# Sums over partitions of modulation products: ones as the moving operand, or the products moving past a pattern of ones

## The chip, the cores and the metric

The kernel runs on one core of one Trainium2 chip. The metric is the device time of one launch in microseconds (us); lower is better. All numbers are fp32; the large matrix products are done in three terms, each operand split into a high part and a low part.

## The reference, cut to what matters

Two transformer blocks run one after the other. The second one is conditioned: in each of its two layers a vector `c` (for the latents) and a vector `c_ctx` (for the context) are multiplied with a large matrix, and the 6144 results of each are the shifts, scales and gates of that layer.

```python
def ada_params(cvec, w, b):                       # w: (1024, 6144)
    return jnp.split(jax.nn.silu(cvec) @ w + b, 6, axis=-1)

for l in range(DEPTH):                            # DEPTH = 2
    sh1, sc1, g1, sh2, sc2, g2 = ada_params(c, ada_w[l], ada_b[l])
    csh1, csc1, cg1, csh2, csc2, cg2 = ada_params(c_ctx, ada_w[l], ada_b[l])
    h_lat = modulate(x, norm_g[l, 0], sh1, sc1)
    h_ctx = modulate(ctx, norm_g[l, 0], csh1, csc1)
    ...
```

The context's last four results of layer 1 are never used, so they are not computed.

## The kernel before

The kernel is one hand-written stream of instructions for each engine, with semaphores between them: `pe.wait_ge(dve_done, at("dve", name))` lets TensorE wait for the VectorE instruction that carries that name. Activations lie feature-major: 128 features on the partitions, tokens along the row.

The feed-forward networks take their weights in chunks through two slots. SyncE loads a chunk into `raw`, ScalarE rounds it to `WH` (line 828), GpSimd forms the rest `WL` (line 757), and TensorE multiplies. A network goes through four quarters of 6, 6, 6 and 4 tiles (`QUARTERS`). In a quarter, each tile has a gate and an up product (`streamed`, lines 2958, 2959, 2963), VectorE multiplies the two to `FH` and `FL` (lines 1782 to 1785), and then eight products of the down projection follow in four steps of two (`lowered`, lines 3178, 3179, 3183, the loop over `k` in steps of 2), whose results VectorE adds up (lines 1796 and 1798).

The modulation vectors are worked out beside two of these networks: layer 0 beside the network `b0`, layer 1 beside the network `t`. Each layer is cut into 12 pieces of 512 result columns (`modulations`: `l`, `block`, and the vectors `vs`). Sixteen pieces are done for both vectors, eight (of layer 1) for one. A piece comes as two halves of the 1024 rows, one DMA of 1 MB each. VectorE multiplies each 128x512 tile by a column of the vector and adds it to `acc` (`modulation`, lines 1756 and 1758), so that 128 partial products for each result remain, one on each partition. TensorE then sums over the partitions (`sums`, line 3114): for each of the 4 blocks of 128 results and each vector, the 128x128 partial products are the stationary operand, and one column of ones moves past them. The result is one column of a PSUM bank, `M[1]` and `S[1]` by turns, results on the partitions, and VectorE adds the bias and writes it to `mod` (`modulated`, line 1771). An fp32 matmul shows as two records in the trace.

The order is fixed by chunk: `half_of` says after which chunk VectorE does which half; TensorE sums piece p after the chunk of the second half of piece p + 1, and the last two pieces of a layer are flushed in the last of the network's quarters that has halves (`flush`), after step `k == 4` of its down projection: quarter 3 for `b0`, quarter 2 for `t`. There, sums of pieces 10 and 11 (22 and 23) are called; piece 10 has been summed by then in `b0`, and piece 22 in `t`.

Of the kernel before, what the change touches and what calls it, by code (L numbers as in the profile page):

```python
# [26 lines left out]
AX = mybir.AxisListType  # L27

P = 128
T = 512  # L30
TC = 256
D = 1024
# [139 lines left out]
def build(nc, a, out, scratch, known):  # L172
# [4 lines left out]
    with ctx:  # L177
# [51 lines left out]
        conv, g_ab, g_qk, gate_b = keep("conv", [P, 3, 4]), keep("g_ab", [P, KD]), keep("g_qk", [P, 2]), keep("gate_b", [16, 1])  # L229
        mlast = keep("mlast", [64, 1])  # L230
        dec = keep("dec", [P, 2, 4])
        mids, steps = keep("mids", [P, 2, T // CHUNK + 2]), keep("steps", [P, 4, TC // CHUNK])
        arena = (cursor[0] + 63) // 64 * 64

# [262 lines left out]
        for name, places in (("b0", (some, most, most, range(4))), ("t", (range(8),) * 3)):  # L497
            for q, slots in enumerate(places):
                for j in slots:
                    half_of[first[f"{name}.gu{q}"] + j] = len(half_of)  # L500
            flush[name, len(places) - 1] = len(half_of) // 2 - 2
        modulations = [(0, b, (0, 1)) for b in range(12)] + [(1, b, (0,)) for b in range(4, 12)] + [(1, b, (0, 1)) for b in range(4)]
        assert len(half_of) == 2 * len(modulations)

        def piece(p):

            return (*modulations[p], (adaw0, adaw1), acc)
# [1161 lines left out]
        def _(dve):  # L1669
# [69 lines left out]
            def modulation(c):  # L1739

                if c not in half_of:
                    return
                h = half_of[c]
                if h % 2 == 0 and h >= 4:
                    modulated(h // 2 - 2)
                l, block, vs, weights, sums = piece(h // 2)
                b = h // 2 % 2
                dve.wait_ge(ada_loaded[h % 2], 16 * (h // 2 + 1))
                dve.wait_ge(dve_done, here())
                for k in range(KD // 2):  # L1750
                    for i, v in enumerate(vs):
                        col = cvec[:, KD // 2 * (h % 2) + k, v:v + 1]
                        if k:
                            dve.wait_ge(dve_done, here() - (len(vs) - 1))
                        if k == 0 and h % 2 == 0:
                            V.tensor_scalar(sums[:, b, i, :], weights[h % 2][:, k, :], col, None, ALU.mult).then_inc(dve_done, did("dve", f"ada.{h}"))
                        else:
                            V.scalar_tensor_tensor(sums[:, b, i, :], weights[h % 2][:, k, :], col, sums[:, b, i, :], ALU.mult, ALU.add)\  # L1758
                                .then_inc(dve_done, did("dve", f"ada.{h}"))

            mods = [0]

            def modulated(p):

                if p < mods[0]:
                    return
                mods[0] = p + 1
                l, block, vs, _, _ = piece(p)
                nv = len(vs)
                dve.wait_ge(pe_done, at("pe", f"ada.sum{p}"))  # L1770
                V.tensor_tensor(mod[:, l, 4 * block:4 * block + 4, vs[0]:vs[0] + nv], (M[1], S[1])[p % 2][:, 0:4 * nv].rearrange("p (b v) -> p b v", b=4),
                                ada_b[:, l, 4 * block:4 * block + 4, vs[0]:vs[0] + nv], ALU.add).then_inc(dve_done, did("dve", f"ada.mod{p}"))

            def feed_forward(n, total, N=T, FH=FH, FL=FL, silu=silu, fresh=False, between=iter(()), last=None):
                for q, count in enumerate(QUARTERS):
# [12 lines left out]
                    for k in range(KD):  # L1788
# [9 lines left out]
                            V.tensor_tensor(total[:, k, :], total[:, k, :], bank, ALU.add).then_inc(dve_done, did("dve", f"{n}.down{q}.{k}"))  # L1798
                        if k % 2 and count == 6:
                            modulation(first[f"{n}.dn{q}"] + k // 2)  # L1800
                        if k == 5 and (n, q) in flush:
                            modulated(flush[n, q])
                            modulated(flush[n, q] + 1)
                        if k % 2:
                            if last and count == 4 and k < KD - 1:
                                for j in EARLY[last].get(k // 2, ()):
# [156 lines left out]
            def bounds_high():  # L1963
# [9 lines left out]
                dve.wait_ge(dve_done, here())  # L1973
                V.tensor_scalar(lb1[:, :, :], lb[:, :, :], -1.0, 1.0, ALU.mult, ALU.add).then_inc(dve_done, did("dve", "lb1"))
                V.tensor_scalar(lbn[:, :, :], lb[:, :, :], -1.0, None, ALU.add).then_inc(dve_done, did("dve", "lbn"))

            def turning():

# [962 lines left out]
        def _(pe):  # L2941
# [160 lines left out]
            def sums(p):  # L3102

                if p < summed[0]:
                    return
                summed[0] = p + 1
                _, _, vs, _, part = piece(p)
                nv = len(vs)
                pe.wait_ge(dve_done, at("dve", f"ada.{2 * p + 1}"))
                if p >= 2:  # L3110
                    pe.wait_ge(dve_done, at("dve", f"ada.mod{p - 2}"))
                for b in range(4):
                    for v in range(nv):
                        last = mm((M[1], S[1])[p % 2][:, nv * b + v:nv * b + v + 1], part[:, p % 2, v, b * P:b * P + P], ones[:, 0:1], start=True, stop=True)
                last.then_inc(pe_done, did("pe", f"ada.sum{p}"))

            def feed_forward(n, N=T, FH=FH, FL=FL, freed=(), between=iter(())):
                X = features(hH, hL, N)
# [9 lines left out]
                for q, count in enumerate(QUARTERS):  # L3128
# [17 lines left out]
                    for k in range(0, KD, 2):  # L3146
# [9 lines left out]
                            tally.also("pe", f"used.{c}")  # L3156
                        if count == 6:
                            sums_after(c)
                        if k == 4 and (n, q) in flush:
                            sums(flush[n, q])  # L3160
                            sums(flush[n, q] + 1)
                        next(between, None)
                for _ in between:
                    pass
# [1031 lines left out]
```

## Time and profile before

| what | value |
|---|---|
| median of 3 runs | 3110.86 us (3107.64 to 3112.96) |
| the profiled execution's own time | 3109.12 us |
| its span, first to last instruction | 3107.3 us |
| mean granted TensorE clock | 0.989 of full speed |
| TensorE busy with matmuls | 3023.5 us, 97% of the span |
| VectorE / ScalarE / GpSimd busy | 55% / 38% / 40% |

The profile is of one execution. PE is TensorE's matmuls, PEld its weight loads, which overlap them, DVE is VectorE, ACT ScalarE, POOL GpSimd. A matmul's duration in the trace runs to the end of its pipeline, so the durations of a stream of matmuls overlap; what one costs is the distance from one to the next, which the chain of work that ended last gives. The page's share of 128x1 matmuls is therefore not what they cost.

### The profile page before, as it was taken

How to read it: one execution, taken by the hardware profiler on the slowest of the kernel's cores; microseconds unless marked ns; L12 is line 12 of the kernel's file. 1: busy time of each engine (PE TensorE's matmuls, PEld its weight loads, DVE VectorE, ACT ScalarE, POOL GpSimd, SP SyncE). 2: the span in 40 equal slices, each digit the busy share in tenths (PEclk: the TensorE clock that was granted, in tenths of full speed). 3: DMA queues.
4: the chain of work that ended last, by engine and by line, in shares of the span. 5: the costliest groups of instructions: out<-in, count | busy, mean ns of one | idle time of the engine just before them, and what ended most of it. 6: DMA issues, size and time to landing. Idle time of an engine off the chain costs nothing.

```text
span 3107.3 us, 41472 instructions
## 1 busy us (share of the span) xinstructions
PE 3023.5 (97%) x16448; PEld 2534.3 (82%) x16448; DVE 1702.9 (55%) x2822; ACT 1182.1 (38%) x1826; POOL 1235.6 (40%) x584
## 2 busy tenths in 40 slices
PE   8999999999999999999999999999999999999999
PEld 7658888886589888778888998878888789878887
DVE  4545676845463553655328866676684457442113
ACT  4643212235445333234336645532223335332222
POOL 4314444533266333333444554444444330244442
PEclk9999999999999999999999999999999999999999
DMA  8214554622245223223333333345653220123331
GB/s 132 65 50 124 166 162 137 182 65 65 70 129 151 83 72 92 82 68 106 112 102 99 113 113 107 128 132 180 190 157 114 76 68 2 41 72 102 99 95 68
DMA packets 480433, 323.87 MB, mean 104 GB/s; under 512 B 102520, under 2 KB 447744, under 8 KB 479728
## 3 DMA queue, kind: packets, MB, share of 16 engines
q1 hardware_dynamic: 475472, 309.60, 34.0%
q10 hardware_dynamic: 2656, 6.30, 0.5%
q0 software_dynamic: 2112, 5.32, 0.5%
q8 instruction: 131, 2.15, 0.3%
q14 instruction: 62, 0.51, 0.1%
HBM read 315.90 MB, written 5.24 MB: 103 GB/s over the span
## 4 chain that ended last, share of the span: by engine, by line
PE 89%; DVE 6%; ACT 2%; issue 1%; POOL 1%; DMA 0%; DVEq 0%; ACTq 0%; POOLq 0%
PE G L2949 13%; PE G L2958 13%; PE G L2959 12%; PE G L2963 12%; PE G L3178 6%; PE G L3179 6%; PE G L3183 6%; PE G L2976 3%; PE G L4097 1%; PE G L3748 1%; PE SS L3306 1%; PE G L3410 1%; PE G L3343 1%; PE SS L2949 1%; POOL WL L757 1%
## 5 line engine op out<-in xcount | busy, mean ns | idle before, releaser
L757 POOL TENSOR_TENSOR WL<-raw,WH 128x1024 fp32r<-128x1024 f32 (+1 forms) x520 | 1192.6, 2316 | 1747.6 <-ACT WH L828 1747.5
L828 ACT ACTIVATE WH<-raw 128x1024 fp32r<-128x1024 f32 (+1 forms) x520 | 492.6, 995 | 596.4 <-PE G L3183 404.2
L2958 PE MATMUL G<-hH,WH 128*128 128x512 f32 x1520 | 595.1, 391 | 0.7 <-ACT xtok L1562 0.7
L2959 PE MATMUL G<-hL,WH 128*128 128x512 f32 x1520 | 591.9, 389 | 0.0
L2963 PE MATMUL G<-hH,WL 128*128 128x512 f32 x1520 | 359.9, 389 | 0.0
L2958 PEld LDWEIGHTS G<-hH,WH 128*128 128x128 f32 x1520 | 285.4, 188 | 61.4 <-ACT xtok L1562 0.9
L2963 PEld LDWEIGHTS G<-hH,WL 128*128 128x128 f32 x1520 | 285.3, 188 | 59.2
L2959 PEld LDWEIGHTS G<-hL,WH 128*128 128x128 f32 x1520 | 285.4, 188 | 58.5
L1758 DVE SCALAR_TENSOR_TENSOR acc<-adaw,cvec,acc 128x512 f32<-128x512 f32 x280 | 280.1, 1053 | 4.2
L1782 DVE TENSOR_TENSOR FH<-silu,G 128x512 fp32r<-128x512 f32 x44 | 30.3, 688 | 245.4 <-PE G L2963 191.0
L2949 PE MATMUL G<-hH,WH 128*128 128x512 f32 (+1 forms) x416 | 161.5, 388 | 0.0
L2949 PE MATMUL G<-hL,WH 128*128 128x512 f32 (+1 forms) x416 | 158.8, 382 | 0.0
L2949 PE MATMUL G<-hH,WL 128*128 128x512 f32 (+1 forms) x416 | 158.8, 382 | 0.0
L3178 PE MATMUL G<-FH,WH 128*128 128x512 f32 x352 | 140.9, 400 | 0.0
L3179 PE MATMUL G<-FL,WH 128*128 128x512 f32 x352 | 138.9, 394 | 0.0
L908 ACT ACTIVATE silu<-G 128x512 f32<-128x512 f32 x44 | 26.4, 600 | 277.9 <-PE G L2963 269.0
L1782 DVE TENSOR_TENSOR m_FH<-m_silu,G 128x512 fp32r<-128x512 f32 x22 | 15.1, 688 | 189.3 <-PE G L2963 183.8
L2949 PEld LDWEIGHTS G<-hL,WH 128*128 128x128 f32 x416 | 80.0, 192 | 15.0 <-issue 0.7
L2949 PEld LDWEIGHTS G<-hH,WH 128*128 128x128 f32 x416 | 79.8, 192 | 14.9 <-issue 0.7
L2949 PEld LDWEIGHTS G<-hH,WL 128*128 128x128 f32 x416 | 79.8, 192 | 14.9
L3183 PE MATMUL G<-FH,WL 128*128 128x512 f32 x352 | 85.8, 391 | 0.0
L2958 PE MATMUL G<-c_nH,WH 128*128 128x256 f32 x336 | 84.2, 290 | 0.0
(825 smaller groups left out, 6040.3 us busy)
## 6 DMA issues: line engine op xcount, KB each, us to landing
raw<-ffn_w_in_in SPq DMA_DIRECT2D x264, 256.0 KB, 3.4
adaw<-ada_w_in SPq DMA_DIRECT2D x48, 1024.0 KB, 5.3
raw<-ab_w_in_in SPq DMA_DIRECT2D x128, 256.0 KB, 3.0
raw<-ffn_w_out_in SPq DMA_DIRECT2D x96, 256.0 KB, 3.0
raw<-w_gate_in SPq DMA_DIRECT2D x88, 256.0 KB, 3.3
raw<-w_up_in SPq DMA_DIRECT2D x88, 256.0 KB, 3.4
raw<-w_down_in SPq DMA_DIRECT2D x64, 256.0 KB, 3.0
raw<-w_in_in SPq DMA_DIRECT2D x40, 256.0 KB, 3.3
```

Source lines behind the costliest of these rows:

```text
L757: nc.gpsimd.tensor_tensor(WL[c % 2][:, cut], raw[c % 2][:, cut], WH[c % 2][:, cut].bitcast(F32), ALU.subtract)\
L828: nc.scalar.activation(WH[c % 2][:, cut], raw[c % 2][:, cut], ACT.Copy).then_inc(weights_hi, 1)
L1758: V.scalar_tensor_tensor(sums[:, b, i, :], weights[h % 2][:, k, :], col, sums[:, b, i, :], ALU.mult, ALU.add)\
L1782: V.tensor_tensor(FH[:, j, :], silu[:, t % 2, :], up, ALU.mult).then_inc(dve_done, did("dve", f"{n}.FH{t}"))
L2949: last = mm(dst, x, y, start=(k == 0 and j == 0), stop=(k == K - 1 and j == 2))
L2958: mm(dst, view(WH[c % 2], k), high, start=(k == 0 and not (joint and i)), stop=False)
L2959: mm(dst, view(WH[c % 2], k), low, start=False, stop=False)
L2963: last = mm(dst, view(WL[c % 2], k), X(k)[0], start=False, stop=(k == K - 1 and not (joint and i == 0)))
L2976: last = mm(dst, x, y, start=(k == order[0] and j == 0 and not (joint and i)), stop=(k == K - 1 and j == 2 and not (joint and i == 0)))
L3178: mm(dst, part(WH, k, cols, o), high, start=(k == 0 and not (joint and i)), stop=False)
L3179: mm(dst, part(WH, k, cols, o), low, start=False, stop=False)
L3183: last = mm(dst, part(WL, k, cols, o), X(k)[0], start=False, stop=(k == count - 1 and not (joint and i == 0)))
```

## The change

A tile `pick` of 128 x 43 elements holds zeros and one column of ones, column 11. Its 32 columns from `11 - block` on are a stationary operand of 32 columns whose column number `block` is ones. The partial products now move: for each vector and each half (256 columns) of a piece, one matmul adds the sums into row `block` of a strip of 32 rows of the bank `M[1]`, and zeros into its other rows. The four strips are (vector, half) = rows 0, 32, 64 and 96. The bank gathers all 12 pieces of a layer; `start` is set on a strip's first piece and `stop` on its last. At the end of a layer VectorE copies the 128x256 bank into `acc` (`modulated_rows`), TensorE turns it with two transposes into `S[1]` (`turned_sums`), and VectorE adds the bias in four instructions (`modulated`). The 24 single additions and their waits are gone; in `b0` the last sums come after step `k == 2` of the down projection and the turn after `k == 4`, in `t` after `k == 4` and `k == 6`.

```diff
+PICKED = 12
+        pick = keep("pick", [P, PICKED + 31])
-            flush[name, len(places) - 1] = len(half_of) // 2 - 2
+            flush[name, len(places) - 1] = (len(half_of) // 2 - 2, 2 if name == "b0" else 4)
 # VectorE
                 if h % 2 == 0 and h >= 4:
-                    modulated(h // 2 - 2)
+                    dve.wait_ge(pe_done, at("pe", f"ada.sum{h // 2 - 2}"))
+            def modulated_rows(p):
+
+                dve.wait_ge(pe_done, at("pe", f"ada.sum{p}"))
+                V.tensor_copy(acc[:, 0, 0, 0:2 * P], M[1][:, 0:2 * P]).then_inc(dve_done, did("dve", f"ada.rows{p}"))
 
             def modulated(p):
 
-                l, block, vs, _, _ = piece(p)
-                nv = len(vs)
-                dve.wait_ge(pe_done, at("pe", f"ada.sum{p}"))
-                V.tensor_tensor(mod[:, l, 4 * block:4 * block + 4, vs[0]:vs[0] + nv], (M[1], S[1])[p % 2][:, 0:4 * nv].rearrange("p (b v) -> p b v", b=4),
-                                ada_b[:, l, 4 * block:4 * block + 4, vs[0]:vs[0] + nv], ALU.add).then_inc(dve_done, did("dve", f"ada.mod{p}"))
+                l = piece(p)[0]
+                pe_name = f"ada.turned{p}"
+                dve.wait_ge(pe_done, at("pe", pe_name))
+                by_block = lambda t: t[:, l, :, :].rearrange("p (b h c) v -> p c v h b", h=2, c=2)
+                for c in range(2):
+                    turned = S[1][:, c * P:c * P + P].rearrange("p (v h b) -> p v h b", v=2, h=2)
+                    for v in range(2):
+                        V.tensor_tensor(by_block(mod)[:, c, v], turned[:, v, :, 0:PICKED], by_block(ada_b)[:, c, v], ALU.add)\
+                            .then_inc(dve_done, did("dve", f"ada.mod{l}"))
 ...
-                        if k == 5 and (n, q) in flush:
-                            modulated(flush[n, q])
-                            modulated(flush[n, q] + 1)
+                        if (n, q) in flush:
+                            p, step = flush[n, q]
+                            if k == step + 1:
+                                modulated_rows(p + 1)
+                            if k == step + 3:
+                                modulated(p + 1)
 ...
+            V.memset(pick[:, :], 0.0).then_inc(dve_done, did("dve", "pick.0"))
+            dve.wait_ge(dve_done, here())
+            V.memset(pick[:, PICKED - 1:PICKED], 1.0).then_inc(dve_done, did("dve", "pick"))
 # TensorE, in sums(p)
                 pe.wait_ge(dve_done, at("dve", f"ada.{2 * p + 1}"))
-                if p >= 2:
-                    pe.wait_ge(dve_done, at("dve", f"ada.mod{p - 2}"))
-                for b in range(4):
-                    for v in range(nv):
-                        last = mm((M[1], S[1])[p % 2][:, nv * b + v:nv * b + v + 1], part[:, p % 2, v, b * P:b * P + P], ones[:, 0:1], start=True, stop=True)
+                chosen = pick[:, PICKED - 1 - block:PICKED + 31 - block]
+                for v in vs:
+                    same = [i for i, m in enumerate(modulations) if m[0] == l and v in m[2]]
+                    for h in range(2):
+                        r = 64 * v + 32 * h
+                        last = mm(M[1][r:r + 32, 0:2 * P], chosen, part[:, p % 2, v, h * 2 * P:h * 2 * P + 2 * P], start=(p == same[0]), stop=(p == same[-1]))
                 last.then_inc(pe_done, did("pe", f"ada.sum{p}"))
+
+            def turned_sums(p):
+
+                pe.wait_ge(dve_done, at("dve", f"ada.rows{p}"))
+                for c in range(2):
+                    last = nc.tensor.transpose(S[1][:, c * P:c * P + P], acc[:, 0, 0, c * P:c * P + P], ident[:, :])
+                last.then_inc(pe_done, did("pe", f"ada.turned{p}"))
 ...
-                        if k == 4 and (n, q) in flush:
-                            sums(flush[n, q])
-                            sums(flush[n, q] + 1)
+                        if (n, q) in flush:
+                            p, step = flush[n, q]
+                            if k == step:
+                                sums(p)
+                                sums(p + 1)
+                            if k == step + 2:
+                                turned_sums(p + 1)
```

## Rows read from the trace of the kernel before

**Rows 1.** The page: span, TensorE's busy time, chain by engine.

```profile
span 3107.3 us, 41472 instructions
PE 3023.5 (97%) x16448; PEld 2534.3 (82%) x16448; DVE 1702.9 (55%) x2822; ACT 1182.1 (38%) x1826; POOL 1235.6 (40%) x584
...
PE 89%; DVE 6%; ACT 2%; issue 1%; POOL 1%; DMA 0%; DVEq 0%; ACTq 0%; POOLq 0%
```

**Rows 2.** Busy time by stretch: networks `b0` and `t`, then a quarter's end.

```profile
core 0: us, PE busy (x) PEld busy (x) DVE busy (x) ACT busy (x) POOL busy (x), PEclk, DMA share, GB/s
225.00:625.00 400.00, 399.46 (x1874) 333.30 (x1873) 282.40 (x332) 98.08 (x122) 178.16 (x85) 1.00 0.51 154
2060.00:2345.00 285.00, 285.00 (x1321) 237.64 (x1320) 209.49 (x235) 64.56 (x81) 127.07 (x56) 1.00 0.58 177
...
420.00:460.00 40.00, 40.00 (x193) 33.44 (x192) 38.67 (x43) 8.75 (x10) 19.09 (x9) 1.00 0.60 178
```

**Rows 3.** Chain, a piece of two vectors: start us, us, what.

```profile
324.70 1.68 PE MM L3114 x16
326.38 0.34 PE G L3178
326.73 0.23 PE G L3179
```

**Rows 4.** Chain, a piece of one vector.

```profile
2110.78 0.79 PE SS L3114 x8
2111.57 0.34 PE G L3178
```

**Rows 5.** Line 3114 by instruction: min/median/max ns, first and last start.

```profile
L3114 PEld LDWEIGHTS MM<-ones,acc x160: 187/192/193, 324.3 to 2335.1; 128*128 128x128 f32 x160
...
L3114 PEld LDWEIGHTS SS<-ones,acc x160: 187/192/193, 342.6 to 2345.2; 128*128 128x128 f32 x160
```

**Rows 6.** Timeline of TensorE: full width, then strips of 64.

```profile
146.94 1.88 PE L3306 MATMUL MM<-kT,qT 128*128 128x512 f32 x4
148.75 1.94 PE L3410 MATMUL G<-pt,vtok 128*64 128x512 f32 x8
```

**Rows 7.** Chain, other fp32 matmuls: 512 columns at full width.

```profile
145.81 1.30 PE SS L3306 x3
```

**Rows 8.** Chain, strips of 64 columns (line 3286), then full width.

```profile
112.64 1.02 PE MM L3286 x16
113.66 0.67 PE G L2949 x2
```

**Rows 9.** Line 3286 by instruction.

```profile
L3286 PEld LDWEIGHTS MM<-w_sT,vg x64: 132/137/137, 110.5 to 734.9; 128*64 128x64 f32 x64
```

**Rows 10.** Timeline of TensorE: 32 rows each, four banks.

```profile
1667.42 0.38 PE L3729 MATMUL SS<-t_va,rstd 32*128 32x128 f32 x2
1667.43 0.38 PE L3729 MATMUL MM<-t_va,rstd 32*128 32x128 f32 x2
```

**Rows 11.** Chain, four transposes inside a stream of matmuls.

```profile
2728.06 0.44 PE G L3055 x4
2728.50 1.16 PE G L2976 x5
```

**Rows 12.** Timelines at the end of `t`, quarter 2.

```profile
2315.55 0.69 DVE L1782 TENSOR_TENSOR t_FH<-ht,G 128x512 fp32r<-128x512 f32 x1 [1.92 <-PE G L2963]
...
2326.53 0.16 DVE L1771 TENSOR_TENSOR mod<-SS,ada_b 128x8 f32<-128x8 f32 x1
2326.80 3.79 DVE L1756 TENSOR_SCALAR acc<-adaw,cvec 128x512 f32<-128x512 f32 x2
...
2336.26 7.07 DVE L1758 SCALAR_TENSOR_TENSOR acc<-adaw,cvec,acc 128x512 f32<-128x512 f32 x8
...
2343.63 1.84 PE L3114 MATMUL SS<-ones,acc 128*128 128x1 f32 x16
```

**Rows 13.** Timelines at the end of `b0`, quarter 3.

```profile
609.80 8.70 DVE L1758 SCALAR_TENSOR_TENSOR acc<-adaw,cvec,acc 128x512 f32<-128x512 f32 x8
...
620.21 0.42 PE L3178 MATMUL G<-FH,WH 128*128 128x512 f32 x1
...
632.33 0.69 DVE L1798 TENSOR_TENSOR xT<-xT,G 128x512 f32<-128x512 f32 x1 [1.54 <-PE G L3183]
```

**Rows 14.** Timeline of VectorE: its first instruction.

```profile
9.12 0.69 DVE L2022 COPY xT<-G 128x512 f32<-128x512 f32 x1 [9.12 <-PE G L3422]
```

**Rows 15.** Groups by line: a copy of the new copy's shape.

```profile
L2912 DVE COPY ptj<-G 128x256 f32<-128x256 f32 x32 | 13.5, 423 | 8.4 <-PE G L4087 6.8
```

More of the change, by code:

```diff
@@ L1759, in modulation @@
                                 .then_inc(dve_done, did("dve", f"ada.{h}"))
-            mods = [0]
+            def modulated_rows(p):
+                dve.wait_ge(pe_done, at("pe", f"ada.sum{p}"))
+                V.tensor_copy(acc[:, 0, 0, 0:2 * P], M[1][:, 0:2 * P]).then_inc(dve_done, did("dve", f"ada.rows{p}"))
             def modulated(p):
-                if p < mods[0]:
-                    return
-                mods[0] = p + 1
-                l, block, vs, _, _ = piece(p)
-                nv = len(vs)
-                dve.wait_ge(pe_done, at("pe", f"ada.sum{p}"))
-                V.tensor_tensor(mod[:, l, 4 * block:4 * block + 4, vs[0]:vs[0] + nv], (M[1], S[1])[p % 2][:, 0:4 * nv].rearrange("p (b v) -> p b v", b=4),
-                                ada_b[:, l, 4 * block:4 * block + 4, vs[0]:vs[0] + nv], ALU.add).then_inc(dve_done, did("dve", f"ada.mod{p}"))
+                l = piece(p)[0]
[7 more added lines that the diff above has]
+                            .then_inc(dve_done, did("dve", f"ada.mod{l}"))
             def feed_forward(n, total, N=T, FH=FH, FL=FL, silu=silu, fresh=False, between=iter(()), last=None):
@@ L3106, in sums @@
                 summed[0] = p + 1
-                _, _, vs, _, part = piece(p)
-                nv = len(vs)
+                l, block, vs, _, part = piece(p)
                 pe.wait_ge(dve_done, at("dve", f"ada.{2 * p + 1}"))
-                if p >= 2:
-                    pe.wait_ge(dve_done, at("dve", f"ada.mod{p - 2}"))
-                for b in range(4):
-                    for v in range(nv):
-                        last = mm((M[1], S[1])[p % 2][:, nv * b + v:nv * b + v + 1], part[:, p % 2, v, b * P:b * P + P], ones[:, 0:1], start=True, stop=True)
-                last.then_inc(pe_done, did("pe", f"ada.sum{p}"))
+                chosen = pick[:, PICKED - 1 - block:PICKED + 31 - block]
[4 more added lines that the diff above has]
+                        last = mm(M[1][r:r + 32, 0:2 * P], chosen, part[:, p % 2, v, h * 2 * P:h * 2 * P + 2 * P], start=(p == same[0]), stop=(p == same[-1]))
+                last.then_inc(pe_done, did("pe", f"ada.sum{p}"))
+            def turned_sums(p):
[3 more added lines that the diff above has]
+                last.then_inc(pe_done, did("pe", f"ada.turned{p}"))
             def feed_forward(n, N=T, FH=FH, FL=FL, freed=(), between=iter(())):
```

## The prediction

> **What bounds the kernel now.** I read the page first, for the engine that is nearly always busy: TensorE, 97% of the span, and 89% of the chain that ended last [rows 1]. An average hides stages, so I then asked for the busy times of the two stretches in which modulation pieces are summed. In `b0` TensorE is busy 399.5 of 400 us, in `t` 285.0 of 285, at a granted clock of 1.00, which is the upper of the two levels (2.4 GHz) [rows 2]. The reader is to see that nothing TensorE waits for shows there: every microsecond less on it is a microsecond less in all, until another engine is late. GpSimd and ScalarE are at half load or less in both stretches; VectorE is at 71 to 74%, but 38.7 of 40 us at the end of a quarter, so it is the one that could be late next.
>
> **What goes.** A matmul of one moving column looks as if it cost nothing. It doesn't: its 128x128 stationary operand has to be loaded, 187 to 192 ns a load [rows 5], and the loads overlap each other only in part. The chain gives what a burst costs: 16 records take 1.68 us, and the matmul behind them 0.34 us where its neighbours take 0.23 [rows 3], together 1.79 us. The bursts of one vector take 0.79 + 0.11 = 0.90 us [rows 4]. There are 320 records [rows 5]: 16 bursts of 16 and 8 of 8. So 16 x 1.79 + 8 x 0.90 = 28.6 + 7.2 = 35.8 us of TensorE go.
>
> **What comes.** A piece of two vectors is now four matmuls (eight records) of 256 moving columns, each into its own strip of 32 result rows; a piece of one vector is two matmuls (four records). An fp32 record of 512 columns takes 1.30 / 3 = 0.43 us [rows 7], so one of 256 takes 0.215 us. Done one behind the other, eight would be 1.72 us, about what goes. All hangs on whether the strips run side by side.
>
> The trace has strips of 64. Four records at full width take 1.88 us from start to end; eight into two strips, with the same 512 columns, take 1.94 [rows 6]. So two strips run at once. It has no strips of 32 result rows, but it has four matmuls of 32 contraction rows each, on four banks, which start within 0.01 us of each other [rows 10]. Two records of each bank stand together only in the merged view; what it shows is that four small matmuls can be in the array at once. I take four strips at once, so two slots of 0.215 us: 0.43 us.
>
> The way in and out costs extra. Line 3286 does 16 records of 128 columns in pairs: eight slots of 0.43 / 4 = 0.108 us are 0.86 us. It takes 1.02 us, and the two matmuls behind it 0.67 us, where two take 0.46 [rows 8]: 1.23 us in all, so 0.37 us for entering and leaving strips. A burst is then 0.37 + 0.43 = 0.80 us, and the same for one vector, whose two strips also need two slots. 24 x 0.80 = 19.2 us. **TensorE gains 35.8 - 19.2 = 16.6 us**, almost all in the 16 large bursts (0.99 each, against 0.10 in the small ones).
>
> The bounds of a burst of two vectors: 0.43 us if entering cost nothing, 0.37 + 8 x 0.215 = 2.09 us if nothing overlapped. I stay at 0.80 since rows 6 and 8 are the nearest in kind: the same two-record fp32 matmuls into strips.
>
> The Trainium skill ("TensorE: Matmul & The Clock Gate", Measured speedup vs the span model) has 3.07x for four row strips and 2.38x for three column strips. By 3.07x, as an estimate, the eight records would take 0.56 us in place of 0.43, and the change would gain 2 us less. The two strips here give 2 x 1.88 / 1.94 = 1.94x.
>
> **The turn.** Two transposes a layer stand in TensorE's stream. Four in such a stream cost 0.44 us, and the matmuls behind run at 0.23 [rows 11]; two are between 0.22 and 0.44. I take 0.3 us, 0.6 for both layers. The copy before them (0.42 us by a copy of its shape [rows 15]) and the four additions (0.16 us each, as the 0.16 of those that go [rows 12]) are VectorE's. In `t` they lie in front of the next quarter. In `b0` VectorE still waits 1.54 us for TensorE behind the place where they are put [rows 13], which covers them; without that cover they would cost 0.42 + 4 x 0.16 - 2 x 0.16 = 0.7 us. The two transposes wait for the copy, but a whole step of the down projection stands between, so I cost that wait at nothing. The memsets of `pick` come while VectorE idles for its first 9.12 us [rows 14]: nothing.
>
> **A stall that appears.** The gain makes TensorE early, and one of its waits has no slack. In `t` the last sums wait for the last half of piece 23. VectorE has worked without a gap since 2315.55 and ends that half at 2336.26 + 7.07 = 2343.33; TensorE's burst starts at 2343.63 [rows 12]. Two bursts lie on TensorE between 2315 and there (pieces 21 and 22), each 0.99 us shorter, so it arrives at 2341.65. VectorE loses the addition at 2326.53, 0.27 us with its distance to the next [rows 12], and is ready at 2343.06. TensorE stands for 1.4 us. Behind the waiting matmuls are step `k == 6` of the down projection and everything after, so this is on the path. In `b0` the sums of piece 11 are moved forward to step 2: TensorE is there at 620.21, after the shorter burst of piece 10 at 619.2; VectorE has the half at 609.80 + 8.70 = 618.50 [rows 13]. 0.7 us of slack, no stall. The removed wait on `ada.mod` never held TensorE, and is worth nothing.
>
> **The sum**: 16.6 - 0.6 - 1.4 = 14.6 us. From the profiled execution's own 3109.1 us that is 3094.5. It lies 1.7 us below the median of the runs, so against the median I forecast **3096 us** (0.5% less).
>
> **Rivals.** (a) *Only two strips at a time.* For: the trace has never more than two column strips at work. Against: rows 10. A large burst is 0.37 + 4 x 0.215 = 1.23 us; TensorE gains 35.8 - 16 x 1.23 - 8 x 0.80 = 9.7 us; the stall shrinks to 0.6; gain 8.5, 3102.
>
> (b) *Loads not hidden.* A load of 64 columns takes 137 ns, of 128 columns 192 [rows 5, 9]: some 0.8 ns a column, 26 ns for 32. If each of eight stood outside, 0.21 us a large burst and 0.10 a small one, 4.2 us in all, with a stall 0.4 us smaller: gain 10.8, 3100. Against: in line 3286 the pairs keep to a slot but for the 0.37 us. The Trainium skill (the same page, Part 3, The mechanism) says that weight loads overlap running matmuls only where the row group differs, which here it never does. By that rule this rival would be the forecast; rows 8 and 9 do not bear it out.
>
> (c) *VectorE gives it back.* At the end of a quarter VectorE is at 38.7 of 40 us [rows 2]. If it also bound the six bursts in or at the end of `b0`'s down projections, 6 x 0.99 = 5.9 us of the gain would go: gain 8.7, 3102. Against: between such stretches VectorE idles, and TensorE's needs there (the additions of two steps before) are old.
>
> (d) *The other side: the strips run one behind the other.* Large bursts 2.09 us, small ones 0.37 + 4 x 0.215 = 1.23: 16 x 2.09 + 8 x 1.23 = 43.3 us, 7.5 more than go, plus 0.6 for the turn: 3119. It decides from the point at which a large burst costs more than 1.79 us. Against it: rows 6, eight records in the time of four.
>
> **Chances.** Forecast 0.60, (a) 0.11, (b) 0.12, (c) 0.09, (d) 0.06, something else of small effect 0.02. The forecast's own spread is some 3 us either way: the runs before spread over 5.3 us, without the stall it is 1.4 less, with free entry up to 6 us less. The range 3090 to 3104 takes in the forecast, (a), (b) and (c) but for their tails, 0.86 together. Some 6 us (0.2%) is about what a measurement of this kernel can tell from no change. Faster by more (below 3104.6): 0.56 + 0.12 + 0.10 + 0.08 and part of the rest = 0.87. Slower: 0.07. Within: 0.06.
>
> **What would show each step.** Bursts of `sums` on the chain: 0.8 us with eight records, and starts of four in one slot; 1.2 is (a), 1.0 is (b), 2.1 is (d). The same for the small ones, 0.8 where 0.9 was. One stall of TensorE of about 1.4 us, in front of the last burst of `t`, released by line 1758; none in `b0`. TensorE otherwise busy throughout both stretches; if it shows waits for line 1782 or 1785 or 1798, (c) is right. The chain between 625 and 640 unchanged but for the missing burst. The forecast is wrong if strips of 32 behave other than strips of 64, or if a change of strips costs TensorE more where it comes from the rounded (fp32r) stream than the 0.37 us read behind line 3281.

## The result and the profile after

The changed kernel takes 3087.74 us (median of 4 runs, 3086.64 to 3091.43), the kernel before in the same session 3111.91 (4 runs, 3107.64 to 3113.55): ratio 0.9927, 95% interval 0.9914 to 0.9940. It is faster by 22.7 us, where 14.6 were forecast, and lies 2.3 us below the range's lower end. The profiled execution took 3086.64 us.

The page of the changed kernel, against [rows 1]: span, busy times, chain by engine.

```profile
span 3084.7 us, 41126 instructions
PE 3001.5 (97%) x16292; PEld 2499.9 (81%) x16292; DVE 1701.9 (55%) x2810; ACT 1183.1 (38%) x1826; POOL 1235.9 (40%) x584
...
PE 88%; DVE 8%; ACT 2%; issue 1%; POOL 1%; DMA 0%; DVEq 0%; ACTq 0%; POOLq 0%
```

TensorE is as much the bound as before; its busy time fell by 22.0 us, the span by 22.6. VectorE's share of the chain rose from 6 to 8%: TensorE now waits for it at two places, shown below, and the chain follows VectorE's work back from each.

The chain of the changed kernel at a piece of two vectors and, further on, at one of a single vector, against [rows 3, 4] (start, us, what):

```profile
421.26 0.57 PE MM L3127 x8
421.83 0.43 PE G L3202
422.26 0.23 PE G L3203
...
2097.76 0.56 PE MM L3127 x4
2098.31 0.43 PE G L3202
```

The eight records take 0.57 us in place of 1.68, and the matmul behind them 0.43 in place of 0.34: 0.57 + 0.43 - 0.23 = 0.77 us a burst, where 1.79 stood. Four records take the same time as eight: 0.76 in place of 0.90. Their records one by one:

```profile
L3127 PEld LDWEIGHTS MM<-acc,pick x160: 105/108/110, 329.0 to 2326.7; 128*32 128x32 f32 x160
L3127 PE MATMUL MM<-acc,pick x160: 379/390/404, 329.0 to 2326.9; 128*32 128x256 f32 x160
```

Eight loads of 0.108 us are 0.86 us, more than the whole burst of 0.77; so the loads too run beside each other. The timeline shows it directly, here for the burst at 421 us, first the loads, then the matmuls:

```profile
421.19 0.16 PEld L3127 LDWEIGHTS MM<-acc,pick 128*32 128x32 f32 x8 [0.35 <-issue]
421.19 0.64 PE L3127 MATMUL MM<-acc,pick 128*32 128x256 f32 x8
```

All eight loads are over 0.16 us after the first began, while the first four matmuls are still running.

The waits of TensorE in `t` (2060 to 2360 us: us in total, times, longest), and the chain there, with the copy and the transposes:

```profile
PE MM L3127 <- DVE acc L1760: 0.7, 1, 0.7
```

```profile
2319.61 7.01 DVE acc L1760 x8
2326.62 0.04 issue
2326.66 0.64 PE MM L3127 x8
2327.30 0.43 PE G L3202
...
2332.96 2.72 PE G L3207 x12
2335.69 0.22 PE SS L3134 x2
2335.91 0.23 PE G L2971
```

This is the one stall that was forecast, at its place, but of 0.7 us. The turn costs its two transposes, 0.22 us, and the matmul behind them takes its usual 0.23.

The timeline of VectorE, and then the chain, of the changed kernel in `b0`, where the last sums were moved forward:

```profile
603.15 8.68 DVE L1760 SCALAR_TENSOR_TENSOR acc<-adaw,cvec,acc 128x512 f32<-128x512 f32 x8
611.94 3.06 DVE L1804 TENSOR_TENSOR xT<-xT,G 128x512 f32<-128x512 f32 x4
614.92 0.42 DVE L1766 COPY acc<-MM 128x256 f32<-128x256 f32 x1
```

```profile
612.73 0.70 DVE xT L1804
613.43 0.04 issue
613.47 0.50 PE G L3202
```

The sums themselves do not wait, as forecast. But the additions to `xT` stand behind those 8.68 us on VectorE, and TensorE's next matmuls need a bank that such an addition frees: TensorE waits 0.3 us for it. This stall was not in the forecast.

### The profile page after: what moved, and what is told of

The parts are those of the page before. It is cut to its first block, busy times and chain, and to the rows that moved or that the text cites. A ratio compares the mean times of both kernels' runs of the same rounds, so it can differ in the third digit from the quotient of the medians.

```text
span 3084.7 us, 41126 instructions
## 1 busy us (share of the span) xinstructions
PE 3001.5 (97%) x16292; PEld 2499.9 (81%) x16292; DVE 1701.9 (55%) x2810; ACT 1183.1 (38%) x1826; POOL 1235.9 (40%) x584
## 4 chain that ended last, share of the span: by engine, by line
PE 88%; DVE 8%; ACT 2%; issue 1%; POOL 1%; DMA 0%; DVEq 0%; ACTq 0%; POOLq 0%
PE G L2962 13%; PE G L2971 12%; PE G L2972 12%; PE G L2976 12%; PE G L3202 6%; PE G L3203 5%; PE G L3207 5%; PE G L2989 3%; PE G L4121 1%; PE SS L3330 1%; DVE acc L1760 1%; PE G L3434 1%; PE G L3367 1%; PE MM L3330 1%; PE SS L2962 1%
## 5 line engine op out<-in xcount | busy, mean ns | idle before, releaser
L1760 DVE SCALAR_TENSOR_TENSOR acc<-adaw,cvec,acc 128x512 f32<-128x512 f32 x280 | 287.3, 1078 | 4.2
```

## The experiments

Eleven kernels were run, each timed against the kernel before on the same chip. Those of one chip are one session: the first four rows, the next four, the last three.

| kernel | median us | before, same chip | ratio, 95% interval |
|---|---|---|---|
| after_again | 3088.61 | 3108.52 | 0.9934 (0.9922 to 0.9945) |
| two_strips | 3100.16 | 3108.52 | 0.9974 (0.9963 to 0.9985) |
| unshifted | 3091.04 | 3108.52 | 0.9940 (0.9927 to 0.9953) |
| pad192 | 3107.68 | 3108.52 | 0.9999 (0.9990 to 1.0008) |
| same_strip | 3116.29 | 3111.26 | 1.0018 (1.0009 to 1.0027) |
| before_again | 3110.57 | 3111.26 | 0.9996 (0.9987 to 1.0005) |
| pad64 | 3115.52 | 3111.26 | 1.0021 (1.0012 to 1.0029) |
| late_last | 3085.64 | 3111.26 | 0.9921 (0.9907 to 0.9934) |
| all64 | 3109.60 | 3110.55 | 0.9999 (0.9988 to 1.0009) |
| pad128 | 3116.59 | 3110.55 | 1.0016 (1.0006 to 1.0026) |
| after_pad128 | 3105.43 | 3110.55 | 0.9979 (0.9970 to 0.9988) |

An interval here is 3 to 4 us either way, and a difference between two sessions is known less well than that. The last part of this section compares the kernels at the same granted clock, which tells more.

The first question was whether four strips side by side give the gain, or something else. The second, once the gain proved larger than its parts, was what else the change moves: `pick` is a new tile of 172 bytes a partition (192 with its rounding), laid out ahead of all working tiles, and shifts every one of them.

**after_again**: the changed kernel, no edit.

> The changed kernel as it is, timed beside the others of this set. Theory A (the gain beyond the forecast 14.6 us is the new place of the tiles and single stretches of half clock that fall differently from run to run): between 18 and 24 us less than before, and against the first profile the half-clock stretches lie elsewhere around the starts of stages. Theory B (the gain is steady and all of it comes from the bursts): 22 to 24 us less each time, with half-clock stretches at the same places.

0.9934, 20.5 us less; with the first session the gain is 20 to 23 us. The bursts in its trace are those of the first one. So the surplus over 14.6 us is not one session's luck, though part of the first 22.7 may be. The half-clock stretches do lie elsewhere in part, as theory A has it.

**two_strips**: two strips of 64 result rows in place of four of 32; the halves of a vector go into the same strip.

```diff
-        pick = keep("pick", [P, PICKED + 31])
+        pick = keep("pick", [P, 43 + 64])
-                        r = 64 * v + 32 * h
-                        last = mm(M[1][r:r + 32, 0:2 * P], chosen, ...
+                        at0 = 43 - 32 * h - block
+                        last = mm(M[1][64 * v:64 * v + 64, 0:2 * P], pick[:, at0:at0 + 64], ...
```

> The changed kernel with two strips of 64 result rows (one for each vector) in place of four of 32: the two halves of a piece go one behind the other into the same strip, through a pattern of 64 columns. Same sums, same placing of the other tiles against multiples of 256 bytes. If the strips run side by side, a burst of two vectors is 0.77 + 2 x 0.215 = 1.20 us and one of one vector 0.37 + 4 x 0.215 = 1.23: in all 24 x 0.43 = 10 us more than the changed kernel, of which the late wait for VectorE in the last burst takes up about 1. If the number of strips did not matter and the gain came from fewer or smaller weight loads, the bursts would stay at 0.8 us and the time within 1 us.

The chain of two_strips, at a piece of two vectors and at one of a single vector:

```profile
418.13 1.02 PE MM L3126 x8
419.15 0.43 PE G L3202
...
2100.86 1.01 PE MM L3126 x4
2101.86 0.43 PE G L3202
```

1.02 + 0.43 - 0.23 = 1.22 us, rival (a)'s 1.23. A single vector's two halves are now in one strip and take as long, 1.21, more than the 0.90 of before. 16 x (1.79 - 1.22) - 8 x (1.21 - 0.90) = 6.6 us less than before; measured are 8.1 (4.7 to 11.5), of which some 2 are the place of the tiles, which is the changed kernel's (below). Against after_again it is 12 us more by the ratios and 9 at the same clock, where 9 to 10 were expected.

**same_strip**: all matmuls of a burst go into one strip (the sums of vectors and halves are mixed, so the modulation values are not the reference's).

```diff
+                turn = p % 12
+                r = 32 * (turn % 4)
-                        r = 64 * v + 32 * h
-                        last = mm(..., start=(p == same[0]), stop=(p == same[-1]))
+                        last = mm(..., start=(turn < 4 and n == 1), stop=(turn >= 8 and n == 2 * len(vs)))
```

> The changed kernel, but the two or four matmuls of a burst all go into one strip of 32 result rows, so that they cannot overlap (the sums of different vectors and halves are mixed, so the modulation values are not the reference's; everything else is as in the changed kernel). Theory (the gain is the overlap of four strips): eight records of 256 columns take 8 x 0.215 = 1.72 us behind each other plus 0.35 for coming and going, a large burst 2.07 us in place of 0.77, a small one 0.35 + 4 x 0.215 = 1.21 in place of 0.755. Against the changed kernel 16 x 1.3 + 8 x 0.46 = 24.5 us more, less 0.8 for the stall of the last burst that goes: about +24, that is 3110 to 3115, no faster than the kernel before. Rival (the gain is the smaller number of records and loads, the strips do not matter): bursts stay under 1 us and the time stays within 4 us of the changed kernel's 3088.

The chain of same_strip at the same two kinds of piece:

```profile
420.49 1.84 PE MM L3129 x8
422.33 0.43 PE G L3205
...
2117.54 0.98 PE MM L3129 x4
2118.52 0.43 PE G L3205
```

1.84 + 0.43 - 0.23 = 2.04 us, where rival (d) said 2.09, and 1.18 for one vector. 16 x 0.25 + 8 x 0.28 = 6.2 us more than before; measured are 5.6 (2.8 to 8.4) more. The form of the matmuls, their count and their loads are those of the changed kernel; only the overlap is gone. From there to after_again it is 1.0018 to 0.9934, 26 us, across two sessions, where 24 were expected. The gain is the overlap. In the same terms, eight records go from 1.84 to 0.57 us, 3.2 times as fast.

**pad192 and unshifted**: the shift without the change, and the change without the shift (`pick` at the top of SBUF, the other tiles where they were).

```diff
+        keep("pad", [P, 43])
         mids, steps = keep("mids", ...
```

```diff
-        pick = keep("pick", [P, PICKED + 31])
+        pick = place("pick", [P, PICKED + 31], F32, top - 192)
```

> The kernel before with nothing but an unused tile of 172 bytes in front of the last two small tiles, so that everything laid out behind them starts 192 bytes later, as in the changed kernel. Theory A: matmuls of 512 columns whose moving operand lies there (FH, FL) go from 229 to 232 ns apart to 226 to 227, those of 256 columns (cH) from 113 to 119 to 120; 2 to 5 us less than before, bursts of ones unchanged at 1.79 us. Theory B: the distances stay and the time is that of before within 1 us.

> The changed kernel with the pattern tile at the very end of the memory, so that every other tile lies where it did before. Theory A: bursts as in the changed kernel (0.77 us), distances of the other matmuls as before (229 to 232 ns for FH, FL); 15 to 19 us less than before and 2 to 5 more than the changed kernel. Theory B: the same time as the changed kernel.

By the times both were inconclusive: by the ratios pad192 is 0.3 us faster than before, where theory A had 2 to 5, and unshifted 1.9 us slower than after_again, each well inside its interval of 3 to 4 us. Unshifted is 18.6 us faster than before, inside the 15 to 19 of its theory A. The traces showed a difference all the same, in opposite directions: the matmuls that read `FH` and `FL` were closer together in pad192, and those of 256 columns that read `cH` were farther apart. Summed start to start over the matmuls that two traces share, without the places where two distances differ by over 80 ns (a wait, or the other clock), pad192 has 3.9 us less in the former and 1.7 us more in the latter than the kernel before, the changed kernel 4.1 less (after_again 3.9) and 1.7 more: 2.3 us net. Hence the next four.

**pad64, pad128, all64, after_pad128**: pad64 and pad128 are pad192 with 16 and 32 columns of `pad`; after_pad128 is the changed kernel with 32 columns of `pad` behind `pick`; all64 shifts every tile, `hH`, `hL` and the weight tiles too.

```diff
-        lowest = (nc.sbuf_base + 63) // 64 * 64
+        lowest = (nc.sbuf_base + 63) // 64 * 64 + 64
```

> The kernel before with 64 bytes a partition laid in ahead of mids: all large tiles behind it start at a multiple of 128 bytes, as in the changed kernel, where before they start 64 bytes behind one. Placement theory: matmuls of 512 columns that read FH and FL follow each other at 226.7 ns in place of a mean of 227.5, those of 256 columns that read cH at 120 ns in place of 113 to 119; net gain 2 us, 0.9993, which a measurement can barely tell. Rival (placement gives the 6 us by which the gain exceeds the bursts' share): ratio 0.998. Rival (it is not the address but the amount, 192 bytes): pitches as in the kernel before.

> The kernel before with 128 bytes a partition ahead of mids: FH, FL and cH start at 64 mod 256 bytes, the fourth of the four places. Theory (what counts is whether the start is a multiple of 64 only or of 128): pitch 229.1 ns as in the kernel before, ratio 1.000. Rival (it grows from 128 over 192 to 0 and stays high): 230 to 233 ns, 1740 x 3 ns = 5 us slower, ratio 1.0015.

> The kernel before with every tile of SBUF 64 bytes further on, hH, hL and the weight tiles too (in pad64 only those behind pad moved). In the traces so far the matmuls of 512 columns that read hH or hL (start 128 mod 256 bytes, some 6160 of them) follow each other at 227.1 ns in every kernel; those that read FH or FL (some 1740) at 229.1 with a start of 192 mod 256, at 226.7 to 227.8 with 128, at 229 to 237 with 0. Theory A (the moving operand's own start address): hH and hL now start at 192, so their pitch becomes 229.1 ns, 6160 x 2 ns = 12 us, and FH and FL start at 0, 9 us as in pad64: 3110 + 21 = 3131, ratio 1.007. Theory B (the distance between the moving operand and the weight tiles): nothing changes, ratio 1.000, pitches as in the kernel before.

> The changed kernel with 128 bytes a partition laid in behind pick: FH, FL and cH start at 0 mod 256 bytes in place of 128. Theory (the start of the moving operand by 256 bytes): the pitch of FH and FL matmuls goes from 227 to 229 to 237 ns as in pad64, 9.1 + 4.4 = 13.5 us by the sums of the two traces, and two thirds of that by the medians of pad64 and pad192; so 3088.6 + 9 to 13.5 = 3098 to 3102, about half of the change's gain gone; bursts as in the changed kernel. Rival (the placing is worth only the 2 us that pad192 showed net): within 4 us of 3088.6.

The stage that shows it best is the down projection of the last network, 36 matmuls of 512 columns for each pair of results: 12 with `m_FH` and the low weights, 24 before them. Two rows of the chain in each, for those 12 records (start, us, what). First before, then all64:

```profile
2997.60 2.75 PE G L3183 x12
3005.84 2.75 PE G L3183 x12
```

```profile
2998.10 2.75 PE G L3183 x12
3006.34 2.75 PE G L3183 x12
```

Then pad192 and the changed kernel:

```profile
3001.70 2.72 PE G L3184 x12
3009.86 2.72 PE G L3184 x12
```

```profile
2983.74 2.72 PE G L3207 x12
2991.89 2.72 PE G L3207 x12
```

Then pad64 and pad128:

```profile
3010.96 2.80 PE G L3184 x12
3019.36 2.80 PE G L3184 x12
```

```profile
2998.31 2.80 PE G L3184 x12
3006.71 2.80 PE G L3184 x12
```

The distance of the two rows is 8.24, 8.24, 8.16, 8.15, 8.40 and 8.40 us; by 36, the matmuls follow each other at 228.9, 228.9, 226.7, 226.4, 233.3 and 233.3 ns (the rows round to 0.01 us, 0.3 ns here; start to start, both kernels of the second pair have a mean of 226.7). Unshifted and after_pad128, whose rows are not shown, have 8.24 and 8.40 us. What orders the six is not the address of the moving tile but its distance to the weight tiles. In bytes modulo 256, start of `m_FH` less start of `WH`:

| distance mod 256 | kernels | ns, from the chain | ratio by time |
|---|---|---|---|
| 0 | pad192, changed kernel | 226.7, 226.4 | pad192 / before 0.9999 |
| 64 | before, all64, unshifted | 228.9 | all64 / before 0.9999 |
| 128 | pad64, after_pad128 | 233.3 | pad64 / before 1.0021, after_pad128 / before 0.9979 |
| 192 | pad128 | 233.3 | pad128 / before 1.0016 |

all64 decides between the two readings. In it `m_FH` starts at the address that it has in pad64, and `hH` and `hL`, which over a third of the kernel's matmuls read, have moved as well; by addresses it should have cost 21 us. It costs nothing, and its pitches (the distances from one matmul's start to the next) are those of the kernel before. So theory B of all64 held. The placement theory of pad64 did not: it had 0.9993, and the kernel became slower, 1.0021. Nor did that of pad128 (1.000 expected, 1.0016 measured); its rival had the time, 1.0015. Both had looked at the address alone.

after_pad128 shows what the place is worth to the changed kernel: 0.9979 against 0.9934, 14 us between two sessions, where 9 to 13.5 were expected. Summed start to start as above, 11.1 us of that are in the matmuls that read `FH`, `FL` and `cH`; the rest goes with the clock (below).

The 256-column matmuls with `cH` go by another pattern. The low-weight matmuls on the chain, before and in the changed kernel:

```profile
943.88 1.81 PE G L2963 x16
963.34 1.89 PE G L2963 x16
```

```profile
934.68 1.92 PE G L2976 x16
940.44 1.92 PE G L2976 x16
```

At the distance 64, 16 take 1.81 or 1.89 us; at 0, 1.92 throughout. Start to start that is 113 to 119 ns, 117 in the mean, against 120. The loads are longer at 0 too; that they set the pace is likely, not shown. The next two views are of before and of the changed kernel, the instructions of `cH`, min/median/max ns:

```profile
L2963 PEld LDWEIGHTS G<-cH,WL x176: 186/188/190, 878.5 to 976.1; 128*128 128x128 f32 x176
```

```profile
L2976 PEld LDWEIGHTS G<-cH,WL x176: 186/192/192, 868.6 to 967.9; 128*128 128x128 f32 x176
```

The Trainium skill ("SBUF — State Buffer", Operand start alignment) asks of an operand only that it start at a multiple of its element size; for whether it may be read that holds in every kernel here, and it says nothing of the time, which these rows show.

**before_again**: the kernel before, no edit.

> The kernel before, once more, for a second trace of it. Ratio 1.000 by every theory. Theory A (where the half-clock stretches of TensorE fall at the starts of stages is chance): between 2700 and 2740 us of the span and between 1670 and 2040 the stretches at half clock differ from those of the first trace by some us in all, and the span lies between 3104 and 3114. Theory B (the change itself moves them): both traces of before have the same 4 half-clock stretches between 2704 and 2738, where the changed kernel's traces have 1 or 2, worth 3.7 us.

Its span is 3104.4 us where the first was 3107.3, with nothing changed. Where TensorE falls to half clock at the start of a stage differs from trace to trace, though these two traces have nearly as much of it in all, 71.3 and 70.2 us. The stretch from 2690 to 2740 us, with the granted clock in the last columns but two, of before, before_again, after and late_last, in that order:

```profile
2690.00:2740.00 50.00, 46.06 (x233) 40.06 (x232) 25.57 (x43) 20.39 (x32) 20.36 (x13) 0.86 0.18 52
```

```profile
2690.00:2740.00 50.00, 45.25 (x231) 38.60 (x231) 24.04 (x41) 23.11 (x35) 19.67 (x12) 0.90 0.18 51
```

```profile
2690.00:2740.00 50.00, 44.78 (x229) 37.22 (x228) 24.05 (x39) 21.31 (x31) 24.41 (x14) 0.97 0.22 64
```

```profile
2690.00:2740.00 50.00, 45.35 (x215) 37.97 (x215) 23.43 (x38) 18.92 (x29) 24.42 (x14) 0.90 0.22 64
```

Between before and after this one place is worth some 3 us, over the whole trace 2.5 (clock 0.9889 against 0.9897). after_again and unshifted also have 0.97 there, two_strips and pad192 have 0.86 like before. Before and before_again differ there, 0.86 and 0.90, so theory B fails as it was put; but so few traces can't tell chance from a tendency. The clocks of all runs can, at the end of this section.

**late_last**: the changed kernel with the sums of piece 23 two steps later (its turn behind the next quarter's first tile, where VectorE idles), and `cH`, `cL`, `ctxT1` 64 bytes further on.

```diff
-        cH, cL, ctxT1, _ = lay(lasting2, ...
+        cH, cL, ctxT1, _ = lay(lasting2 + 64, ...
                             if k == step:
                                 sums(p)
+                            if k == step + 2 * (n == "t"):
                                 sums(p + 1)
-                            if k == step + 2:
+                            if k == step + 2 and n != "t":
                                 turned_sums(p + 1)
...
+                        if n == "t" and j == 0 and (n, q - 1) in flush:
+                            turned_sums(flush[n, q - 1][0] + 1)
```

(VectorE's copy and additions move with them.)

> The changed kernel with two edits. The sums of piece 23 stand two steps later in t, with its copy, transposes and additions in or behind the first gate and up tile of the next quarter, where VectorE idles 10 us: the stall of 0.75 us in front of the last burst goes. And cH, cL and ctxT1 start 64 bytes later, so that the 256-column matmuls follow each other at 113 to 119 ns again in place of 120: 2.5 us. Theory: 3.2 us faster than the changed kernel (0.9990 of it), about 3085. Rival: TensorE's wait moves to another place (copy or transposes waited for) or the 2.5 us are not the address's: no difference from the changed kernel.

The chain of late_last at the place of the stall, and one row of its 256-column matmuls:

```profile
932.91 1.81 PE G L2978 x16
...
2329.64 2.72 PE G L3212 x12
2332.36 0.57 PE MM L3129 x8
2332.93 0.43 PE G L2973
```

TensorE waits for nothing in `t` any more, and the 16 take 1.81 us again; start to start, 0.76 us less at the last burst and 1.9 less in the matmuls with `cH` and `cL` than in the changed kernel. Both mechanisms did what was expected. By the times, late_last is the fastest version here, 0.9921 of before, but 0.9921 and after_again's 0.9934 have overlapping intervals, and the two did not run on the same chip at the same time. At the same clock it is 4.9 us faster, known to some 2, where 3.2 were expected.

**The granted clock of the runs.** Every timed run has its mean granted clock on record, to 0.001. Over the 88 runs of the kernel before in the three sessions (the 11 of before_again among them) the times scatter by 3.6 us around 3110.6, and the longer ones are those with the lower clock (correlation 0.91): a straight line through them falls by 2.6 us for each 0.001 of clock, and around it the scatter is 1.5 us. So two kernels can be compared at the same clock: each 0.001 that one has more is counted as 2.6 us that it would otherwise take longer. This is worked out from recorded runs, and is not an experiment. The means of each kernel and of before in the same session:

| kernel | its clock, before's | us against before | us against before at the same clock |
|---|---|---|---|
| after_again | 0.9894, 0.9876 | -20.8 | -16.2 |
| unshifted | 0.9890, 0.9876 | -17.8 | -14.2 |
| pad192 | 0.9875, 0.9876 | -0.7 | -1.1 |
| two_strips | 0.9878, 0.9876 | -8.0 | -7.4 |
| same_strip | 0.9868, 0.9869 | +5.4 | +5.2 |
| pad64 | 0.9886, 0.9869 | +5.6 | +10.1 |
| late_last | 0.9884, 0.9869 | -24.9 | -21.1 |
| all64 | 0.9874, 0.9871 | -1.0 | -0.3 |
| pad128 | 0.9896, 0.9871 | +4.8 | +11.4 |
| after_pad128 | 0.9867, 0.9871 | -6.6 | -7.5 |

The 95% intervals of the last column are 0.9 to 1.4 us either way, 2.1 for late_last; the slope was fitted to the kernel before, and within the other kernels it is nearer 2.2 us, which would make after_again -16.9 and pad128 +10.4.

Two things follow. The granted clock is not the same for all kernels: the nine runs of the changed kernel in two sessions have 0.9893 in the mean and none under 0.988, the 88 of before 0.9872, which is too far apart for chance. It is some 66 us at the lower level against 80. And it does not go with speed or with short bursts: pad128, slower than before, has the highest clock, and after_pad128, with the changed kernel's bursts, the lowest. What decides it was not tried. At the same clock the placing shows in the times as well: pad192 is 1.1 us faster than before (0.2 to 2.0), unshifted 2.0 us slower than after_again. From 64 to 128 costs 10 us (pad64), from 0 to 128 some 9 (after_pad128 less after_again, across two sessions); the second ought to be the larger by 1 or 2, so such a comparison is good to some 3 us.

## Why the prediction was wrong

The mechanism of the change was right; what the sum left out was larger than what it had wrong. The steps in order:

**What goes and what comes.** Forecast 0.99 us a large burst and 0.10 a small one, 16.6 us. Measured 1.02 and 0.14: 17.4 us. The slot and the 0.37 us for coming and going, both read from strips of 64 in another stage, held to 0.03 us for strips of 32. Rival (b), by which the loads would not be hidden, had 1.0 us for a large burst; 0.77 was measured, with all eight loads over in 0.16 us. The Trainium skill's rule that a load overlaps running matmuls only where the row group differs ("TensorE: Matmul & The Clock Gate", Part 3, The mechanism) does not fit these eight records, which all take all rows and differ in their columns alone. Rivals (a) and (d) did not happen, but their prices for a large burst were right once they were built: 1.22 for 1.23 and 2.04 for 2.09 us. That two_strips also took 3100.2 us where (a) had 3102 is luck in part: it is not quite (a), as its small bursts cost 1.21 us in place of 0.80, 3.3 us in all, and the place of its tiles gave some 2 back. same_strip took 3116.3 for 3119.

**The turn.** Forecast 0.6 us, measured 2 x 0.22 = 0.4.

**The stall in `t`.** Forecast 1.4 us, measured 0.7. VectorE was expected to lose one addition, 0.27 us, of its way to the last half. From its row at `t_FH` to the end of that half it took 27.8 us before [rows 12] and 26.6 after, so 1.2 less. Most of that is the first write into `acc` behind the addition that goes: 3.79 us before [rows 12], 2.75 us after, and the second traces of both kernels have 3.78 and 2.75. Why those two instructions became shorter was not tried.

**No stall in `b0`.** Wrong by 0.3 us. The forecast looked at what the moved sums wait for and had 0.7 us of slack right; it did not look at what stands behind VectorE's half of a piece, the additions that free TensorE's banks. That is rival (c) in small.

These steps give 17.4 - 0.4 - 0.7 - 0.3 = 16.0 us, where 14.6 were forecast. Added up burst by burst, start to start, the trace gives the same: 35.8 us before, 19.3 with both stalls after, 0.4 for the turn. With these sizes right the forecast would have been 3095, well inside its range.

**The placing.** The prediction costed `pick` by its two memsets, "nothing". A new tile ahead of the others also moves them, here by 192 bytes: 2.3 us less by the distances between matmuls in the traces, 1.1 and 2.0 by the times of pad192 and unshifted at the same clock. The effect is shown (pad64, pad128, all64, after_pad128); its size in this change is 1 to 2 us. That would have made some 3093, still inside the range.

**The step that failed** is a term that the sum does not have: the granted clock of the whole kernel. The prediction read it as 1.00 in the two stretches and took what TensorE saves there off a time of the kernel before, as if the clock elsewhere stayed what it was; for the scatter of the runs it had 3 us either way. The changed kernel's runs have a mean granted clock of 0.9893 against 0.9872, in the second session 0.9894 against 0.9876, and 0.0018 at 2.6 us for each 0.001 are 4.6 of the 20.8 us there. At the same clock the change gains 16.2 us (15.3 to 17.1), near the 14.6 of the forecast, and 3110.9 - 16.2 = 3094.7 lies inside the range; the clock took the time out of it. Why the clock is higher stays open; unshifted has the higher clock too, so it is not the place of the tiles alone, and after_pad128 has not, so it is not the bursts alone. The experiments do not go further.

The account is not closed to the last microsecond: steps and placing by the traces give 16.0 + 2.3 = 18.3 us, 1 to 2 more than the times at the same clock. Of the 22.6 us between the two spans, 2.5 are clock and 1.8 are left over, mostly waits at the starts of stages; by 2.9 us the two spans of the unchanged kernel differ too.

## What to carry to other kernels

Sums over partitions whose results are few were cheaper here when the data moved and a narrow pattern of ones stood: four strips of 32 result columns ran at once, and the price was the 0.35 us of coming and going, about the same for two strips as for four. The number of strips decides: with one, the same matmuls cost more than the columns of ones that they replace. When a stream is bound by matmuls, count in every edit that adds or resizes an SBUF tile what it does to the distances between the moving tiles and the weight tiles behind it; a pad of 64 to 128 bytes cost 10 us here, more than half of what the change gains. When work is moved forward on one engine, check the banks that the next matmuls need, not only the wait of what is moved. And when a change of some tenths of a percent is judged, put the mean granted clock of the runs beside their times: a difference of 0.002 went with 5 us here, and came with edits made for other ends.

## What the runs showed of the hardware

- The pace of fp32r matmuls depends on where the moving tile lies relative to the stationary one, modulo 256 bytes: 226.7 ns at 0, 228.9 at 64, 233.3 at 128 and 192, for 512 columns in the last network's down projection. At 128 that is a mean of unequal ones: start to start, 237 ns with `m_FH` and the high weights and 229 with `m_FL`. Shifting both together changes nothing. Only these four distances, with these tiles, were seen.
- For 256 columns the order is another: 113 to 119 ns at a distance of 64 (117 in the mean), 120 at 0, with the weight loads 188 and 192 ns long in the median.
- Four fp32 matmuls of 32 result columns, each of two records, run beside each other although all use all rows: eight records in 0.57 us on the chain, where in one strip they take 1.84. Their loads do too, eight in 0.16 us.
- Leaving such strips costs the next full-width matmul 0.43 us in place of 0.23 on the chain, whether the burst had one strip, two or four.
- The mean granted clock of this program differs from kernel to kernel by more than the scatter of its runs, 0.9867 to 0.9896, and from run to run of one kernel the time falls by 2.6 us for each 0.001 of it (88 runs).
